# A two-network kernel: one table set for the roots of the norms, two norms of x from one root, split weights and products in another order

## What is computed

```python
def rmsnorm(x, g):
    y = x * lax.rsqrt(jnp.mean(x * x, axis=-1, keepdims=True) + EPS)
    return y * g

def first_block(...):                     # DEPTH = 1
    mod = c_act @ w_ada + b_ada           # sh1, sc1, g1, sh2, sc2, g2
    h = rmsnorm(x, norm1_g) * (1.0 + sc1) + sh1
    ...                                   # hgrn2 and sparse attention on h @ w_in
    x = x + g1 * (jnp.concatenate([o_hg, o_nsa], axis=-1) @ w_out)
    h = rmsnorm(x, norm2_g) * (1.0 + sc2) + sh2
    x = x + g2 * moe_ffn(h, ...)          # 64 experts, 8 per token, and a shared one
    return rmsnorm(x, final_g)

def second_block(...):                    # DEPTH_2 = 2
    for l in range(DEPTH_2):
        h = rmsnorm_2(x, g_norm[l, 0]) * (1.0 + mod[:, 1]) + mod[:, 0]
        x = x + 0.5 * mod[:, 2] * swiglu_2(h, w_ffn1_gu[l], w_ffn1_down[l])
        h = rmsnorm_2(x, g_norm[l, 1]) * (1.0 + mod[:, 4]) + mod[:, 3]
        x = x + mod[:, 5] * hybrid_mixer(h, ...)
        h = rmsnorm_2(x, g_norm[l, 2]) * (1.0 + mod[:, 7]) + mod[:, 6]
        x = x + 0.5 * mod[:, 8] * swiglu_2(h, w_ffn2_gu[l], w_ffn2_down[l])
    return rmsnorm_2(x, g_final)
```

## Time and profile before

| what | value |
|---|---|
| median of 3 runs | 3216.39 us (3215.98 to 3220.06) |
| profiled execution | 3212.0 us, span 3210.0 us |
| PE busy | 3032.6 us (94%), 13728 matmuls |
| DVE busy | 1681.7 us (52%) |
| ACT busy | 1132.7 us (35%) |
| POOL busy | 368.8 us (11%) |
| DMA | 554.53 MB, mean 173 GB/s |
| granted TensorE clock, mean | 0.974 |

### The profile page before, as it was taken

One profiled execution on the slowest core, in us unless ns is written; L12 is line 12 of the kernel. 1 busy time (PEld: TensorE's weight loads), 2 busy tenths in 40 slices (PEclk: granted clock), 3 DMA queues, 4 the chain that ended last, 5 costly groups with the idle time before them and its releaser, 6 DMA issues. The chain is left out here.

```text
span 3210.0 us, 38633 instructions
## 1 busy us (share of the span) xinstructions
PE 3032.6 (94%) x13728; PEld 2340.0 (73%) x13728; DVE 1681.7 (52%) x1825; ACT 1132.7 (35%) x1331; POOL 368.8 (11%) x424
## 2 busy tenths in 40 slices
PE   5999996999999997899999999999999999999998
PEld 4876564666777665688877778888788877778886
DVE  6744645777777764655226565532655236543323
ACT  3123533556555551422125432212322135332222
POOL 0100001244544430000000000000000000000000
PEclk9998998999999998999999999999999999999999
DMA  7552215899999976455222145432544222122321
GB/s 263 175 188 82 73 33 201 335 355 356 370 360 347 357 297 256 157 183 183 94 78 106 54 144 184 184 113 82 183 183 170 92 95 79 66 79 93 103 92 66
DMA packets 115272, 554.53 MB, mean 173 GB/s; under 512 B 20593, under 2 KB 22130, under 8 KB 72946
## 3 DMA queue, kind: packets, MB, share of 16 engines
q1 hardware_dynamic: 88690, 490.39, 41.6%
q0 software_dynamic: 26496, 62.96, 5.7%
HBM read 548.06 MB, written 37.75 MB: 182 GB/s over the span
## 5 line engine op out<-in xcount | busy, mean ns | idle before, releaser
L176 ACT ACTIVATE stream_high<-stream_raw 128x2048 fp32r<-128x2048 f32 x156 | 298.7, 1915 | 806.2 <-PE ffn_ps_psum L544 760.9
L542 PE MATMUL ffn_ps_psum<-h_high_f,stream_high 128*128 128x512 f32 x1408 | 553.4, 393 | 24.8 <-DVE h_low_f L250 24.8
L181 DVE TENSOR_TENSOR stream_low<-stream_raw,stream_high 128x2048 fp32r<-128x2048 f32 x156 | 356.7, 2286 | 379.1 <-ACT stream_high L176 375.7
L544 PE MATMUL ffn_ps_psum<-h_high_f,stream_low 128*128 128x512 f32 x1408 | 550.4, 391 | 0.0
L543 PE MATMUL ffn_ps_psum<-h_low_f,stream_high 128*128 128x512 f32 x1408 | 550.4, 391 | 0.0
L294 DVE TENSOR_TENSOR weights_low<-weights_raw,weights_high 128x2048 fp32r<-128x2048 f32 x128 | 293.4, 2292 | 183.9 <-ACT weights_high L290 183.8
L542 PEld LDWEIGHTS ffn_ps_psum<-h_high_f,stream_high 128*128 128x128 f32 x1408 | 266.2, 189 | 83.1 <-issue 28.0
L544 PEld LDWEIGHTS ffn_ps_psum<-h_high_f,stream_low 128*128 128x128 f32 x1408 | 265.8, 189 | 56.3
L543 PEld LDWEIGHTS ffn_ps_psum<-h_low_f,stream_high 128*128 128x128 f32 x1408 | 266.4, 189 | 55.0
L290 ACT ACTIVATE weights_high<-weights_raw 128x2048 fp32r<-128x2048 f32 x128 | 244.2, 1908 | 144.7 <-PE experts_g_psum L544 144.7
L542 PE MATMUL ffn_ps_psum<-ffn_hid_high,stream_high 128*128 (+1 forms) x704 | 277.5, 394 | 3.2 <-DVE ffn_sg L738 3.2
(11 more groups left out here) (413 smaller groups left out, 4673.5 us busy)
## 6 DMA issues: line engine op xcount, KB each, us to landing
weights_raw<-in_exp_gu SPq DMA_DIRECT2D x128, 1024.0 KB
stream_raw<-in_ffn_gu SPq DMA_DIRECT2D x88, 1024.0 KB
weights_raw<-in_exp_dn SPq DMA_DIRECT2D x64, 1024.0 KB, 7.7
con<-in_w_mod SPq DMA_DIRECT2D x120, 512.0 KB, 5.7
stream_raw<-in_ffn_dn SPq DMA_DIRECT2D x44, 1024.0 KB
mix_mod_rows<-in_w_ada POOLq DMA_DIRECT2D x32, 512.0 KB, 4.8
...
```

The lines of the kernel that those rows point to most:

```text
L176: self.nc.scalar.activation(self.high[:, q], self.raw[:, q], ACT.Copy).then_inc(self.high_done, 1)
L181: self.nc.vector.tensor_tensor(self.low[:, q], self.raw[:, q], self.high[:, q].bitcast(F32), ALU.subtract)\
L542: mm(out, w[0], x[0], start=start, stop=False)
L544: return mm(out, w[1], x[0], start=False, stop=stop)
```

## The change

1. **One table set.** `natural_log_exp_and_others` holds both Ln and Exp; it is loaded ahead of the first square.
2. **Apply.** Eight buffers: DVE makes all eight xn, then all eight lows. PE's first piece (`multiply_first`) takes for each k both products with `h_high`, for two banks, and after all k the 16 matmuls with `h_low`.
3. **Second weight piece.** Both first pieces of a stage are split in the stage before. DVE makes the low part of the first ahead of the additions to xT, and high (a cast) and low of the second behind them (`split_both`). In `start` ACT and DVE split both. The loops of the feed-forward are turned so that the split of the second slot stands at the end of a round's body. In ffn12, which has no other work in that loop, ACT's table load for Silu now falls into the loop.
4. **Items loop.** Ln and Exp per head straight from PSUM, at the four items where the copy was; the block at i == 14 goes.
5. **between goes.** With x1 = x·r·g (r the first root) the second norm needs mean(x1²) = r²·mean(x²g²), and the product of both roots is 1/sqrt(mean(x²·(g² + eps)) + eps²). `combine` makes `gain` = sqrt(g² + eps) and `pre` = (1 + scale)·next_g·g, and ACT squares gain·x per 128x128 tile behind each addition. For token tiles 0 and 1 DVE reduces over features ahead of a matmul; for 2 and 3 PE sums eight. Ln and Exp then come for 384 and for 128 tokens. SP loads ffn00's first two pieces ahead of the last token tile's rows; ACT splits their high parts at tile 2, DVE the lows around the last `into_x`. Rows of odd token tiles land in tiles of their own, in part that of the shared expert's weights, once those are used.
6. **late=True in ffn00.** xT itself is normed by final_g beside the last two up pieces.

```diff
     def square(self, act, n):
+        if n == 0:
+            self.nc.scalar.preload_act_table_set(LOG_EXP)
...
+    def split_both(self, dve, n):
+        q = self.slot(n)
+        dve.wait_ge(self.loaded[q], 16 * ((self.base + n) // 2 + 1))
+        self.nc.vector.tensor_copy(self.high[:, q], self.raw[:, q]).then_inc(self.high_done, 1)
+        self.split_low(dve, 0, n)
...
+    def multiply_first(self, pe, banks, part):
+        for k in range(KD):
+            pe.wait_ge(self.high_done, k + 1)
+            for u, bank in enumerate(banks):
+                w = part(k, u)
+                mm(bank, w[0], high[:, k, :], start=k == 0, stop=False)
+                mm(bank, w[1], high[:, k, :], start=False, stop=False)
+        last = []
+        for k in range(KD):
+            pe.wait_ge(self.low_done, k + 1)
+            for u, bank in enumerate(banks):
+                last.append(mm(bank, part(k, u)[0], low[:, k, :], start=False, stop=k == KD - 1))
...
                     root.before(dve)
+                    if next_w:
+                        split(ALL // 2, 1)
                     for n in range(KD):
...
                     if next_w:
-                        split(ALL // 2, 1)
+                        w.split_both(dve, ALL + 1)
...
                             for piece, r in ((0, 2 * g), (4, 2 * g + 1)):
-                                split(r, 1)
                                 mod.multiply(dve, g, (piece, piece + 1))
                                 finish(r, 0)
                                 split(r + 1, 0)
                                 mod.multiply(dve, g, (piece + 2, piece + 3))
                                 finish(r, 1)
+                                split(r + 1, 1)
...
+                    def late_root():
+                        r = late_rstd
+                        nc.scalar.preload_act_table_set(LOG_EXP)
+                        act.wait_ge(late_summed, 1)
+
+                        act.wait_ge(w.used, w.base + FT)
+                        nc.scalar.activation(r, ps[:, 6, :], ACT.Ln, bias=self.eps[:, 0:1], scale=1.0 / D).then_inc(late_logged, 1)
...
+                                if late and first and a == 0 and n == 6:
+                                    pe.wait_ge(late_logged, 1)
...
-                                copy_misc(at[:, (i - 7) // 2, :], f"ss{(i - 7) // 2}", S)
-                        if i == 14:
-                            act.wait_ge(misc_free, misc["ss3"] + 1)
-                            a(flat(at[:]), flat(at[:]), ACT.Ln, bias=self.eps[:, 0:1], scale=1.0 / P).then_inc(logged, 1)
-                            act.wait_ge(logged, 1)
-                            a(flat(at[:]), flat(at[:]), ACT.Exp, scale=-0.5).then_inc(rooted, 1)
+                                hd = (i - 7) // 2
+                                act.wait_ge(misc_done, misc[f"ss{hd}"] + 1)
+                                a(at[:, hd, :], bank(MISC), ACT.Ln, bias=self.eps[:, 0:1], scale=1.0 / P).then_inc(misc_free, 1)
+                                act.wait_ge(misc_free, misc[f"ss{hd}"] + 1)
+                                a(at[:, hd, :], at[:, hd, :], ACT.Exp, scale=-0.5).then_inc(rooted, 1)
...
+                        if c == LAST:
+                            for n in range(2):
+                                w.load(sp, n, n, next_w[n])
                         for j in range(TOPK):
...
+                    for c in range(TT):
+                        if c == 2:
+                            for n in range(2):
+                                w.split_high(act, 0, n)
+                        for n in range(KD):
+                            act.wait_ge(added, KD * c + n + 1)
+                            a(sq[:, n, cols(c)], xT[:, n, cols(c)], ACT.Square, scale=gain[:, n:n + 1]).then_inc(weighed, 1)
...
-        k.between(then(0, 0))
+        k.moe((raw, high, low), then(0, 0))
```

301 lines of the change are left out of this document (173 added, 128 removed).

## The result

The changed kernel took 3186.99 us in the median of 4 runs (3183.2 to 3191.26), the kernel before beside it 3218.22 (3215.98 to 3225.35): a ratio of 0.989, 95% interval 0.9871 to 0.9909, 31 us less. The profiled execution of after took 3191.26 us with a span of 3189.5; that of before had 3210.0. So the two spans lie only 20.5 us apart, and where the rest went has to be explained too.

A forecast was written before the change was run, and what follows sets the result against it. PE, busy 3032.6 of 3210.0 us, was taken as the bound, so only its stops and the end could move the time. Terms summed to -31.9 us, giving a median of 3184.5, range 3171 to 3200.

The forecast's parts named there:

- start: Beginning of the kernel: first low half sooner, PE starting at 47.3 instead of 47.44; -0.1 us (-1 to +1.2).
- items loop: First mixer: the ACT block and PE's 4.5 us stall go, with slow clock behind; -5.5 us (-3 to -7.5).
- root ahead of routing: The mixer's root before the routing takes less time; -1.3 us.
- combine and norm: Combine to ffn00: the stage between goes, PE starts feed-forward at 1285.5 instead of 1302.12; -16.6 us (-12 to -19.5).
- norm beside ffn00: Norming x beside ffn00's last two up pieces costs one sum on PE; +0.9 us, +3 if both covers fail.
- five borders: Stage borders of the second network: load gone -1.3, earlier PE start -0.83, first sum +0.5 each; -8.0 us (-4 to -10).
- store: The last root, at the store, gets shorter with nothing behind it to take that back; -1.3 us.
- the last rows' delay: In combine, 2.1 MB of weights queued ahead make the last rows and sums 5.3 us later; bound 8 us.
- A: Borders: shorter PE idle no longer lowers the clock, saving 10 us more, 3174.5; chance 0.10.
- B: Seven roots: a table switch costs more than its row, at most 6 us more saved, 3178.5; chance 0.05.
- C: Thin covers: cast 2.29 (+4.0), combine gives only 12 (+4.6), items loop only 3 (+2.5); 3195.6, chance 0.20.
- D: Rotated feed-forward loops make PE wait in 44 rounds, deciding from 0.87 us a round; 3241 at 1.28, chance 0.03.

The follow-up runs named there:

- e1: The changed kernel run once more with nothing altered, for a second trace; median 3194.95 us, ratio to before 0.9921.
- e11: The changed kernel run a third time with nothing altered; median 3180.78 us, ratio to before 0.9871.
- e4: Changed kernel with the items loop as before: a copy per head and one block of Ln, load and Exp at item 14; median 3186.22 us.
- e7: Changed kernel without the norm of x beside ffn00's last two up pieces, so the output is wrong; median 3185.24 us.
- e3: Changed kernel without the table load ahead of the squares, so six roots load for Ln and for Exp again; median 3187.72 us.
- e6: Changed kernel with DVE making xn and low in turns and PE taking a tile's three products together; median 3197.44 us.
- e2: Changed kernel with combine's last rows loaded ahead of the weights, tile 1's reduce as PE sums, piece 1 split in ffn00; median 3175.41 us, ratio 0.986.
- e9: e2 plus ACT making piece 0's high half, the reduce back on DVE, PE's first feed-forward sum one output later; median 3174.44 us, ratio 0.9845.
- e10: Changed kernel with the low half of the next stage's first piece back behind DVE's additions to xT; median 3199.22 us.

## Why the prediction was right

The median came 2.5 us above the forecast of 3184.5, inside the range, and 31.2 of the forecast 31.9 us went. That this is so close is partly luck: beside the kernel before, the changed one was 31.2, 24.4 (e1) and 41.0 us (e11) faster in three sets of runs, with medians of 3186.99, 3194.95 and 3180.78; the first mixer's clock alone moves single traces by up to 16 us. All three medians lie in the range. The terms, read from the stages, don't depend on that stretch:

| term | forecast | measured | from |
|---|---|---|---|
| start | -0.1 | +0.2 | means of the first row of the table |
| items loop | -5.5 | -5.1 | stretch of 80 us, means; e4 has 78.9 again |
| root ahead of routing | -1.3 | -1.2 | 60.35 before, 59.11 after, from the matmul at 431.66 of before to the routing's first |
| combine and norm | -16.6 | -14.8 to -15.4 | 86.14 to 71.32, 70.69 and 71.10; no run puts `between` back |
| norm beside ffn00 | +0.9 | +0.9 | e7, and PE's row |
| five borders | -8.0 | -7.9 | 1893.7 to 1886.1 without the clock, less the 0.9 and the store; by length -8.3, -5.5 (e1) and -8.3 (e11) |
| store | -1.3 | -0.6 | 379.76 to 379.15 |
| sum | -31.9 | about -29 | |

**Borders.** Idle fell from 5.96, 6.64, 6.05, 5.95 and 6.15 to 3.92, 4.08, 3.99, 3.88 and 4.08. The forecast said about 3.9. Its two parts stand alone in e3 (1.28) and e6 (0.79), as idle and, without the clock, as time. The bound on the cast that I took, the one-operand row, was right at 1.22. The first pair's wait was 0.37 as idle time on PE; in mix0 the changed kernel's lead over before falls from 14.65 us to 14.00 behind the first sum, so it costs 0.65, with 0.5 forecast. The differences of the stages themselves go from 0.34 (ffn10) to 2.34 (mix0), since the clock in them changed too: 1.5 lost became 2.8 in ffn10, 2.6 became 1.7 in mix0.

**Combine.** The step that was mis-sized is the last rows' delay, and it is most of why the term fell short: 7.2 us, where the weights by the queue's rate gave 5.3. e2 measures the weights at 5.6. The other 1.6 is there in e2 as well; in that trace DVE had no idle from 1250.8 on and the first reduce stood ahead of it with 1.91, but whether that is also the cause in the changed kernel, where DVE waited 3.81 for the rows, no run tells. A reduce took 1.89, and not 1.2: the strided read was in the bounds. From there the total held, not each step: PE started 13.2 us after the last sums, where 13.3 was forecast, with the reduce 0.7 longer and the way from the last addition to PE 0.5 shorter (5.0 against 5.5).

**Small terms.** The items loop came near its -5.5 with its parts otherwise split: the stall less what Ln and Exp cost is 4.4 and not 3.5, and the clock gave 0.7 between the means and not 2. Store gave 0.6 of 1.3. The normed tiles start 0.92 us behind Exp (0.82 before), and from there to the end it takes 9.4 us and not 8.9; why the output takes half a microsecond more is open.

**The rivals.** A, the clock kept at full speed behind the shorter idle, did not come: from ffn00 on 14.2 us were lost to it before, and 13.7, 16.7 and 13.7 after. In e2 ffn00 began with 3.38 of idle and lost nothing, in e9, with the same 3.38, 1.7. B, the dearer switch, fell with e3. C, thin covers, did not come, but its ground was real: the cover on DVE is only 0.17 us, and e10 shows what is behind it. D fell: ffn02 is 1.35 us shorter, where its border (-2.06), the first sum (+0.65) and the clock (-0.3) make -1.7, and ffn10 0.34, where the same three (-2.07, +0.65, +1.3) make -0.1; what is left for the turned loops is 0.4 us in a stage at most, not 0.87 in a round. No run turns the loops back, and none puts ACT's split of the second piece back among the highs; that these cost and gain nothing more follows only from the sum of the borders (-7.9 against -8.0).
